# First block: transfers reordered, the bias of the third head group made by small products, bias table read in place, one normalisation written by two engines

## The reference, cut to what matters

```python
h = rmsnorm(x, g_norm_mix) * (1.0 + sc1) + sh1           # sc1, sh1 from cond @ w_ada
c_q, c_kv, k_pe, dil, gates = split(h @ w_in)
o_a = mla_attention(c_q, c_kv, k_pe, ...)                 # 8 heads
for gi, (win, dd) in enumerate(((128, 1), (512, 4), (2048, 16))):
    o_g, lse_g = dilated_band_attention(dil[gi], positions,
                                        rel_bias[:, 8 * gi:8 * gi + 8], win, dd)
# in it:  bias = bias_table[t5_bucket(rel)]; s = s + bias; masked to the band
x = x + gt1 * ((g_a * o_a + g_b * o_b) @ w_out)
x = x + gt2 * expert_choice_ffn(rmsnorm(x, ...), ...)     # 16 experts
```

## Time and profile before

| | |
|---|---|
| median of 3 runs | 2698.93 us (2697.22 to 2700.38) |
| the profiled execution | 2699.61 us, span 2697.7 us |
| PE busy | 2246.9 us (83% of the span) |
| DVE busy | 937.2 us (35%) |
| ACT busy | 367.8 us (14%) |
| DMA | 638.01 MB, mean 237 GB/s |
| mean granted TensorE clock | 0.917 of full speed |

### The profile page before, as it was taken

One profiled execution on the slowest core, in us unless ns is written; L12 is line 12 of the kernel. 1 busy time (PEld: TensorE's weight loads), 2 busy tenths in 40 slices (PEclk: granted clock), 3 DMA queues, 4 the chain that ended last, 5 costly groups with the idle time before them and its releaser, 6 DMA issues.

```text
span 2697.7 us, 29005 instructions
## 1 busy us (share of the span) xinstructions
PE 2246.9 (83%) x11524; PEld 1590.1 (59%) x11524; DVE 937.2 (35%) x2315; ACT 367.8 (14%) x743; POOL 1.2 (0%) x16
## 2 busy tenths in 40 slices
PE   3989987987766776666666699998999988899998
PEld 2767876863222222222222388777888877788886
DVE  6698799121000100000010215724322325333223
ACT  2222111120000000000000112211110114111111
POOL 0000000000000000000000000000000000000000
PEclk8989998998787878888888799999999999999999
DMA  7424563448999999999999943025444422354420
GB/s 261 144 94 176 199 217 95 187 187 338 427 428 428 429 428 428 429 429 428 428 429 429 371 156 125 1 67 178 161 156 155 153 85 78 126 187 156 155 93 16
DMA packets 146959, 638.01 MB, mean 237 GB/s; under 512 B 10037, under 2 KB 52542, under 8 KB 118974
## 3 DMA queue, kind: packets, MB, share of 16 engines
q1 hardware_dynamic: 145876, 634.28, 60.0%
q10 hardware_dynamic: 1002, 2.61, 0.3%
HBM read 635.82 MB, written 1.05 MB: 236 GB/s over the span
## 4 chain that ended last, share of the span: by engine, by line
PE 62%; DMA 24%; DVE 11%; ACT 2%; issue 1%; ACTq 0%; SPq 0%; DVEq 0%
DMA arena<-in_w_down_dram 22%; PE PS L1476 16%; PE PS L1489 8%; PE PS L926 8%; PE PS L1007 8%; DVE arena L1565 7%; PE PS L1328 4%; PE PS L1230 3%; PE PS L1319 2%; PE PS L1355 2%; PE PS L937 2%; PE PS L1342 2%; PE PS L1238 1%; DVE arena L1561 1%; DVE rstd L1574 1%
## 5 line engine op out<-in xcount | busy, mean ns | idle before, releaser
L1476 PE MATMUL PS<-hT,arena 128*128 128x256 f32 x2048 | 445.9, 380 | 2.9 <-DVE hT L1565 2.9
L1328 PE MATMUL PS<-arena,hT 128*32 128x512 f32 x2048 | 306.9, 742 | 160.8 <-DMA arena<-in_w_up_dram 134.6
L1476 PEld LDWEIGHTS PS<-hT,arena 128*128 128x128 f32 x2048 | 390.0, 191 | 57.0 <-issue 3.8
L1328 PEld LDWEIGHTS PS<-arena,hT 128*32 128x32 f32 x2048 | 65.8, 124 | 383.3 <-DMA arena<-in_w_up_dram 211.9
L1565 DVE SCALAR_TENSOR_TENSOR arena<-arena,tiny 128x128 f32<-128x128 f32 (+2 forms) x752 | 281.0, 448 | 0.0
L1007 PE MATMUL PS<-hT,arena 128*128 128x256 f32 (+1 forms) x1136 | 256.8, 387 | 18.0 <-DMA arena<-in_w_in_dram 18.0
L1342 PE MATMUL PS<-arena,hT 128*32 128x512 f32 x1024 | 171.6, 805 | 101.6 <-DMA arena<-in_w_down_dram 94.9
L1007 PEld LDWEIGHTS PS<-hT,arena 128*128 128x128 f32 (+1 forms) x1136 | 216.1, 192 | 57.4 <-DMA arena<-in_w_in_dram 18.2
L1562 DVE TENSOR_SCALAR arena<-arena,cols 128x256 f32<-128x256 f32 x162 | 66.3, 409 | 463.0 <-ACT arena L858 382.9
L1489 PE MATMUL PS<-arena 128*128 128x256 f32 x1024 | 223.3, 379 | 0.0
L926 PE MATMUL PS<-hT,arena 128*128 128x256 f32 x960 | 209.5, 381 | 6.1 <-DVE hT L1565 6.1
(11 more groups left out here) (234 smaller groups left out, 1646.8 us busy)
## 6 DMA issues: line engine op xcount, KB each, us to landing
arena<-in_w_gate_dram SPq DMA_DIRECT2D x64, 2048.0 KB, 40.9
arena<-in_w_up_dram SPq DMA_DIRECT2D x64, 2048.0 KB, 40.7
arena<-in_w_down_dram SPq DMA_DIRECT2D x64, 2048.0 KB, 38.2
arena<-in_ffn_w_up_dram SPq DMA_DIRECT2D x32, 2048.0 KB, 8.7
arena<-in_w_in_dram SPq DMA_DIRECT2D x36, 1024.0 KB, 7.7
arena<-in_ffn_w_down_dram SPq DMA_DIRECT2D x16, 2048.0 KB, 7.8
arena<-in_w_ada_dram SPq DMA_DIRECT2D x12, 2048.0 KB, 11.4
arena<-in_ssd_w_in_dram SPq DMA_DIRECT2D x10, 2048.0 KB, 12.2
```

The lines of the kernel that those rows point to most:

```text
L1328: mm = pe.matmul(PS[32 * f:32 * f + 32, 1 + half, :], xe[:, 32 * (2 * pi + k):32 * (2 * pi + k) + 32], w[:, k, 512 * f:512 * f + 512], sta ...
L1476: mm = pe.matmul(PS[:, n, T * half:T * half + T], slot(TAIL_SLOT[j], 8, 512)[:, k, P * n:P * n + P], hT[:, k, :], start=(k == 0), stop=(k ...
```

## The change

Five things are done.

1. SP issues `const` and the seven early rows first, then `w_ada`, then the first four weight panels, and the 23 small loads only behind these; the second `uq` panel follows them. ACT issues only positions, `x`, mask, table, and the new small inputs `spread` and `table4`. The turn of the small rows of the second block (`rows_turn`) moves on PE from ahead of tile 10 to behind tile 34, and their copies on ACT behind tile 37. The first expert panel is loaded in the middle of the dilated panels, behind a wait for `s_read`.
2. The third group's bias is no longer accumulated on DVE. PE turns its bucket numbers (L1015 of the changed kernel, inside the `w_ada` products), spreads them over partitions by four products (L1052), DVE compares them with the row number (`far_hot`), and PE multiplies that by the table in 32 products of 32 rows and 8 columns (L1066). ACT copies the result (`far_bias`).
3. Bucket 16 is left out: 31 buckets a pass.
4. `entry` is gone: the table's column is the scalar operand itself.
5. ACT and DVE write four pieces each of `hT`.

The diff, cut to its core:

```diff
+BUCKET_IDS = [b for b in range(BUCKETS) if b != BUCKETS // 2]
+N_BUCKETS = len(BUCKET_IDS)
...
+            sp.dma_start(const[:, :], A["shape_const"]).then_inc(s["const_loaded"], 16)
+            for piece in PIECES[:EARLY]:
+                sp.dma_start(*row_piece(*piece)).then_inc(s["early_loaded"], 16)
             for j in range(4):
                 load_ada(j)
+            load("mla_in", 0, at("mla_in", 0, 8, Q_RANK), w_in[:, :, 0:Q_RANK])
+            load("mla_in", 1, at("mla_in", 1, 8, 320), w_in[:, :, COL_KV:COL_DIL])
+            load_gates(0)
+            load("uq", 0, at("uq", 0, 3, 768), w_uq[:, :, 0:768])
             for piece in PIECES[EARLY:]:
                 small(*row_piece(*piece))
...
+            for j in range(18):
+                load_dil(j)
+                if ada_after(j) is not None:
+                    load_ada(ada_after(j))
+                if j == 13:
+                    sp.wait_ge(s["s_read"], 12)
+                    expert_panel(0, 0, 0)
...
+            act.dma_start(spread, A["spread"]).then_inc(s["bias_in"], 16)
+            for j in range(4):
+                act.dma_start(table4[32 * j:32 * j + 32, :],
+                              A["rel_bias"][:, 2 * HEADS:3 * HEADS]).then_inc(s["bias_in"], 16)
...
-            for k in range(KD):
+            for k in range(0, KD, 2):
                 act.activation(by_class_out(hT[:, k, :]), by_class(sq[:, k, :]), ACT.Identity,
...
+            act.wait_ge(s["far_out"], 4)
+            act.activation(far_bias.rearrange("p (i j h) -> p j i h", j=4, h=HEADS),
+                           PS[:, 0:4, 0:64].rearrange("p j (i h) -> p j i h", h=HEADS), ACT.Copy
+                           ).then_inc(s["far_ready"], 1)
...
             for j in range(4):
+                if j == 3:
+                    pe.wait_ge(s["near_ready"], 1)
+                    for c in range(TC):
+                        mm = pe.transpose(PS[0:16, 2, P * c:P * c + P], bucket[:, c, T + 64:KC], ident)
+                    mm.then_inc(s["far_t"], 1)
                 ada_rows(j)
...
+                    pe.wait_ge(s["far_bt"], 1)
+                    for m in range(4):
+                        mm = pe.matmul(PS[:, m // 2, T * (m % 2):T * (m % 2) + T],
+                                       spread[:, P * m:P * m + P], far_bucket, start=True, stop=True)
...
+            pe.wait_ge(s["far_hot"], 2)
+            for i in range(2 * 4):
+                for j in range(4):
+                    r = slice(32 * j, 32 * j + 32)
+                    mm = pe.matmul(PS[:, j, HEADS * i:HEADS * i + HEADS],
+                                   far_hot[r, i % 4, P * (i // 4):P * (i // 4) + P], table4[r, :],
+                                   start=True, stop=True)
...
             def bias_hot(n):
-                b = n % BUCKETS
-                dve.tensor_copy(entry[n % 2], table[:, b * (GROUPS * HEADS):(b + 1) * (GROUPS * HEADS)])
-                ts(onehot[n % 2], bucket, iota[:, b:b + 1], None, ALU.is_equal).then_inc(s["bias_hot"], 1)
+                b = BUCKET_IDS[n % N_BUCKETS]
+                ts(onehot[n % 2], bucket[:, :, 0:T + 64], iota[:, b:b + 1], None, ALU.is_equal
+                   ).then_inc(s["bias_hot"], 1)
...
-                for g in range(GROUPS):
+                for g in range(2):
...
+            dve.memset(tiny[:, 119:120], 0.0).then_inc(s["near_ready"], 1)
             bias_hot(0)
+            dve.wait_ge(s["far_t"], 1)
+            dve.tensor_copy(far_bucket, PS[0:16, 2, 0:T]).then_inc(s["far_bt"], 1)
...
+            for k in range(1, KD, 2):
+                ts(by_class_out(hT[:, k, :]), by_class(sq[:, k, :]), A1[:, k:k + 1], mod[:, k:k + 1], ALU.mult,
+                   ALU.add).then_inc(s["h1_dve"], 1)
+            for i in range(2):
+                dve.wait_ge(s["far_ps"], i + 1)
+                ts(far_hot[:, 2 * i:2 * i + 2, :], PS[:, i, :].rearrange("p (m t) -> p m t", t=T), bucket_row, None,
+                   ALU.is_equal).then_inc(s["far_hot"], 1)
...
                 if q < 2:
-                    for n in range(step + 6, step + 16):
+                    for n in range(step + 6, step + 16 - q):
```

More of the change, by code:

```diff
@@ L302, in program @@
         lg, aff = (view(tiny, 128 + 32 * i, 2, 16) for i in range(2))
-        entry = [tiny[:, 192 + 32 * u:192 + 32 * u + GROUPS * HEADS] for u in range(2)]
+        table4 = tiny[:, 192:200]
         dskip = tiny[:, 256:272]
@@ L316, in program @@
         xtok = view(arena, S6, 2, D)
-        rows = view(arena, S6 + 4096, N_TILES, P)
+        rows = view(arena, MISC, N_TILES, P)
         qn, kn = view(arena, S6, 8, T), view(arena, S6 + 2048, 8, T)
@@ L337, in program @@
         gbT = view(arena, MISC, 8, T)
-        bucket, *onehot = (view(arena, MISC + 2048 + 2 * KC * i, 2, KC) for i in range(3))
-        fold_tmp = arena[:, MISC + 2048 + 4 * KC:MISC + 2048 + 4 * KC + P]
+        bucket = view(arena, MISC + 2048, 2, KC)
+        onehot = [view(arena, MISC + 2720 + 640 * i, 2, T + 64) for i in range(2)]
+        fold_tmp = arena[:, MISC + 3360:MISC + 3360 + P]
+        spread = arena[0:16, S4 + 7 * 1024:S4 + 7 * 1024 + 512]
+        far_hot = view(arena, MISC + 1024, 4, T)
+        far_bucket = arena[0:16, MISC + 7904:MISC + 8160]
+        far_bias = arena[:, MISC + 8160:MISC + 8416]
+        far = far_bias.rearrange("p (c j h) -> p c h j", c=TC, h=HEADS)
         table = arena[:, MISC + 4064:MISC + 4832]
@@ L470, in _ @@
                 load_gates(j)
-            for j in range(18):
-                load_dil(j)
-                if ada_after(j) is not None:
-                    load_ada(ada_after(j))
-            for j in range(2):
-                load("out", j, at("out", j, 4, D), w_out[:, 4 * j:4 * j + 4, :])
             def expert_panel(e, j, r):
@@ L487, in expert_panel @@
                 sp.dma_start(dst, src).then_inc(slot_in[si], 16)
+            for j in range(18):
[5 more added lines that the diff above has]
+                    expert_panel(0, 0, 0)
+            for j in range(2):
+                load("out", j, at("out", j, 4, D), w_out[:, 4 * j:4 * j + 4, :])
             p0 = ST.first["moe"]
-            for q in range(RING_MOE):
+            for q in range(1, RING_MOE):
                 phys = MOE_SLOT[q]
@@ L581, in _ @@
             act.dma_start(posi, bass.AP(A["positions"].tensor, 0, [[0, P], [1, T]])).then_inc(s["pos_loaded"], 16)
-            for piece in PIECES[:EARLY]:
-                act.dma_start(*row_piece(*piece)).then_inc(s["early_loaded"], 16)
-            act.dma_start(const[:, :], A["shape_const"]).then_inc(s["const_loaded"], 16)
             for c in range(TC):
@@ L702, in _ @@
                 evac(34 + i, gaT[:, 4 + i, :])
+            act.wait_ge(s["rows_t"], 2)
+            cols_copy(2, range(1, 4))
+            act.wait_ge(s["rows_t"], 3)
+            cols_copy(3, range(4, N_TILES))
             def exps(a):
@@ L1044, in _ @@
             gate_tile(9)
-            pe.wait_ge(s["small_loaded"], 16 * (len(PIECES) - EARLY + 4))
-            rows_turn(1, range(1, 4))
-            rows_turn(2, range(4, N_TILES))
             pe.wait_ge(s["h_ready"], 1 + 3)
@@ L1083, in _ @@
                 gate_tile(t)
+                if t == 34:
+                    pe.wait_ge(s["small_loaded"], 16 * (len(PIECES) - EARLY + 4))
+                    rows_turn(2, range(1, 4))
+                    pe.wait_ge(s["std_ready"], 2)
+                    rows_turn(3, range(4, N_TILES))
             def mla_scores(a):
@@ L1617, in _ @@
             dve.memset(tiny[:, 118:119], 0.0).then_inc(s["pos_done"], 1)
-            dve.wait_ge(s["bias_in"], 32)
+            dve.wait_ge(s["bias_in"], 112)
             for c in range(TC):
@@ L1765, in _ @@
                     bias_add(16 + a, 1)
-            for n in range(24, BUCKETS):
+            for n in range(24, N_BUCKETS):
                 bias_add(n)
@@ L2114, in shape_constants @@
     put("token", r[:, None])
+    put("bucket_row", r[:, None] % 32)
     put("same_expert", r[:, None] % 32 == np.arange(16)[None, :])
@@ L2152 @@
         give(name, inputs[name])
-    for name, a in zip(("shape_const", "dil_mask"), shape_constants()):
+    for name, a in zip(("shape_const", "dil_mask", "spread"), shape_constants()):
         give(name, a)
```

66 lines of the change are left out of this document (34 added, 32 removed).

## The result

The changed kernel takes 2652.39 us (median of 4 runs, 2649.91 to 2655.34) against 2699.65 for the kernel before (4 runs beside it): 0.9825 of its time, 95% interval 0.9808 to 0.9842, 47 us faster. Predicted were 2654 and a range of 2640 to 2669.

The account below looks back on a forecast made before the run. The prediction took the first block as bound by DVE's bias additions and the expert stage by its transfers, each microsecond won before the router counting fully. Terms summed to 44.7 us, giving 2654 us (range 2640 to 2669).

Parts of the forecast that it names:

- The start: Up to the first projection: new load order brings it from 57.96 to 35.3 us, 22.6 us earlier.
- The sign of being wrong: In the profile after: a first projection later than 40 us would prove the prediction wrong, as would PE waiting for `uq`.
- The small products: Added work on PE: 64 records at 7.0 us and four spreading products at 1.7, together 8.7 us lost.
- The rule of the Trainium skill: On PE's 32-row products: four on different row groups run at once, 3.07 times as fast; 2.3 us instead of 7.0.
- The MLA: Around the first MLA turn: DVE wait and half clock go, less a 1.9 us wait for ACT; 9.6 us won.
- DVE's bucket: DVE's bias additions: one bucket falls from 5.04 to 4.28 us, 0.76 less.
- rounds 0 and 1: Dilated rounds q = 0 and 1: cheaper buckets leave 4.5 us of the 17.9 us wait; 21.2 us won.
- The sum: Whole kernel: 22.6 - 8.7 + 9.6 + 21.2 = 44.7 us won.
- The expert stage: Rival: expert transfers, not the router, set the stream's start, so the end stays at 2699; chance of no change 0.02.
- The start did gain less: Rival: loads come 10 us later than reckoned, start wins 12, 2664 us; chance 0.20, shared with a dearer bucket.
- The small products did overlap: Rival: products overlap or PE's clock stays full, saving up to 2 to 5 us, 2650; chance 0.13.
- The slower rival: Small loads delay the second `uq` panel beyond ten microseconds to spare, lost one for one; slower than before, chance 0.05.

Follow-up runs that it names:

- three_ahead: Changed kernel with three buckets of heads 4 to 7 added in DVE's idle stretch before the first dilated maximum, not at the end of round q = 1; 2645.17 us.
- tiny_more: Changed kernel with four more pairs of loads of 16 values a partition among the small loads, ahead of the second `uq` panel; 2713.13 us (three executions).
- far_one_group: Changed kernel with the 32 small products reordered so that eight in a row use the same group of 32 rows; 2664.57 us.
- order_only: Changed kernel with the bias made as before (32 buckets, three groups, table row copied, no small products); new load order kept; 2670.0 us.
- bias_only: Changed kernel with the loads in the order of before; new bias, later row turns, split norm and early expert panel kept; 2673.98 us.
- near_late: Changed kernel with the two far transposes and their wait for DVE's bucket numbers moved behind the last `w_ada` panel; 2657.36 us.
- norm_one: Changed kernel with `hT` written by ACT alone again, eight pieces in a row; 2650.84 us.
- all_warm: Changed kernel with far transposes later, ACT's row copies earlier, three buckets moved ahead of round q = 0, plus zero products in PE's start waits; 2650.07 us.

## Why the prediction was right

**The start: 22.6 predicted, 17.8 measured.** The term that failed is the time from `x` to the first projection. `x` came at 10.97, not 10.0 (1.0). From there to the near numbers it took 22.5 us, not 20.3: the square sums took 5.51 us against 3.72 before. The last `w_ada` panel ran at half clock, 3.19 us for 1.8 (1.4), where I had counted nothing for the clock "as PE waits in between again". The rest is 0.2. The 1.8 us of the square sums come with the execution, not with the change: in three_ahead and tiny_more, the same code up to there, the sums took 3.72, `x` to the near numbers 20.7 us, and the start won 20.1. The gate that the sum counted as costless is costless there (the panel starts at 31.6 and 31.8 us there, and at 31.4 to 31.7 in the traces without the gate that have fast sums; I had put its landing at 30); in the changed kernel's trace it passed on the late sums and held the panel until 34. The sign of being wrong, a first projection after 40 us, came true by 0.1 us in this trace and not in those two.

**The small products: 8.7 predicted, 3.8 measured.** The four spreading products cost 1.9 to 2.0 (1.7 priced). The 64 records cost 1.9, not 7.0. The row taken as the nearest, L1319, has other products, and far_one_group shows why it misled: one after the other they cost 8.60 us, some 5.7 of it at full clock; in turn on four groups of rows they overlap. The 1.9 us run from the first of the 64 records to the next tile, so the change from 128 rows to 32 and back is in them. The rule of the Trainium skill that stood beside the sum was right, and the estimate by it, 2.3, near the 1.97.

**The MLA: 9.6 predicted, 10.6 measured** (24.6 at the first dilated scores, less 17.8, plus 3.8). The first turn waits for nobody and the wait of 1.80 us for ACT was foreseen as 1.9. But the cause was told too narrowly: order_only, without any cheaper bucket, already has 5.8 us of it. Its first turn waits 1.22 us for DVE, not 7.26, since PE is itself later by the wait for ACT and a tile at half clock (6.37 us for 3.72), and 3.9 us are won behind the turn, where nothing runs at half clock any more.

**DVE's bucket: 4.28 predicted, 4.29 measured; rounds 0 and 1: 21.2 predicted, 22.3 measured** (259.6 - 237.4, before rounding). The turn of round 1 waits no more, from it to the turn in round 2 are 78.6 us (78.8 predicted), and that wait is 4.29 (4.5 predicted). bias_only shows this term alone, with the same 22.3, and three_ahead that the rest of the wait was DVE's.

**The sum: 44.7 predicted**, 46.9 at the last dilated scores, 46.4 at the first expert product, 44.1 at the end of the profiled executions and 47.3 by medians. Two terms were off by nearly 5 us each, with opposite signs: that the total is nearer than its parts is luck.

**The rivals.** The expert stage passed the gain on. The start did gain less, by 5 us rather than 10, but only 1.0 of it by a late load, which was this rival's reason. The small products did overlap. The slower rival didn't come to pass, by a margin of some 19 us where I had 10; its price of the small loads was pessimistic: issued from 37.7 us on, they and the stall were over at 67, in 29 us where I had 45.

What stays open is the square sums' 5.51 us, which follow below, and the 3 us between the profiled executions and the medians.

## What to carry to other kernels

Price a wait by where its lateness is forgiven: an engine that idles at a later meeting point doesn't hand its backlog on, so gains before and after such a point add up, and two changes that remove the same wait don't. Small products cost little when successive ones stand on different groups of rows, and 4.4 times as much when they don't (half clock included), so the order of two loops was worth 9 of the 12 us that far_one_group lost. Keep loads of single values out of a stream that someone needs soon (9.5 us each here), and where one engine waits late and idles early, move its work, which gave 6 to 7 us for three lines. Before reading 2 us out of the marks of two traces, look whether a stretch that is the same in both took the same time in both.

## What the runs showed that I had not expected

- A load of 16 scattered values on 64 partitions, 4 KB in all, costs 9.5 us of the whole queue (76 us for eight), with 0 GB/s and a DMA share of 0.05 for that time.
- The granted clock fell to half inside the 64 serial products (0.83, then 0.50) with PE busy without a break, and fell behind a wait of 1.8 us in near_late, order_only and far_one_group, but not behind the same wait in the changed kernel, three_ahead, norm_one, bias_only and tiny_more. Such a drop is worth about 3 us here, as much as the changes in question; what decides it no run here shows.
- The 16 square sums took 5.20 to 5.91 us in four traces (changed, norm_one, far_one_group, all_warm) and 3.72 in the eight others, with a granted clock of 1.00 in each. In all_warm PE had been at work without a break since 9.1 us but for 1.2 us, so it isn't PE's wait for `x` that makes them slow. The column doesn't tell these apart, and the cause stays open.
